# Splitting one 2 MB weight load of a two-layer encoder block into twelve transfers of few rows

## The reference, cut to what matters

```python
def clamped_swiglu(h):
    glu, lin = jnp.split(h, 2, axis=-1)
    ...
    return glu * jax.nn.sigmoid(SWIGLU_ALPHA * glu) * (lin + 1.0)

    def expert_block(args):
        xb, e = args
        return clamped_swiglu(xb @ w1[e] + b1[e]) @ w2[e] + b2[e]
...
h = layer_norm(DEEPNORM_ALPHA * x + mix, ln1_w, ln1_b)
ffn = moe_ffn(h, router_w, router_b, moe_w1, moe_b1, moe_w2, moe_b2)
return layer_norm(DEEPNORM_ALPHA * h + ffn, ln2_w, ln2_b)
```

## Time and profile before

| | |
|---|---|
| median of 3 runs | 1308.47 us (1308.01 to 1309.79) |
| profiled execution, its own time | 1308.29 us |
| its span, first to last instruction | 1306.5 us |
| PE busy | 1251.2 us, 96% of the span |
| read from main memory | 457.54 MB, 351 GB/s over the span |

### The profile page before, as it was taken

The page is one execution under the profiler, slowest core; times in us unless marked ns, Lnnn a source line. Parts: engine busy times, 40 slices in busy tenths (PEclk is TensorE's granted clock), DMA queues, the critical chain, the costliest instruction groups (busy, mean ns, idle before and its releaser), DMA issues.

```text
span 1306.5 us, 15013 instructions
## 1 busy us (share of the span) xinstructions
PE 1251.2 (96%) x6078; PEld 637.7 (49%) x6078; DVE 453.9 (35%) x911; ACT 218.9 (17%) x427; POOL 3.5 (0%) x17
## 2 busy tenths in 40 slices
PE   9999999999999999999998999999999899999995
PEld 8888888998753333433333333333333333333331
DVE  4999915456357132121221212122121212122123
ACT  1622124131041101101011010101101010111101
POOL 0000000000000000000000000000000000000000
PEclk9999999999999999999999999999999999999999
DMA  9443334326779899999999999999999999999995
GB/s 369 176 158 129 128 131 164 125 98 237 288 306 420 358 433 432 432 431 430 428 430 430 431 431 431 430 431 432 431 432 432 431 429 430 429 432 428 428 424 222
DMA packets 29277, 459.53 MB, mean 352 GB/s; under 512 B 4480, under 2 KB 4864, under 8 KB 9248
## 3 DMA queue, kind: packets, MB, share of 16 engines
q1 hardware_dynamic: 25936, 454.04, 83.1%
q10 hardware_dynamic: 3280, 4.56, 1.1%
HBM read 457.54 MB, written 1.05 MB: 351 GB/s over the span
## 4 chain that ended last, share of the span: by engine, by line
PE 67%; DMA 21%; DVE 9%; ACT 1%; issue 1%; SPq 0%; DVEq 0%
DMA store<-in_moe_w 21%; PE banks L1189 16%; PE banks L796 15%; PE banks L1219 12%; PE banks L810 4%; PE banks L1195 3%; DVE store L1854 2%; PE banks L1071 2%; PE banks L1276 2%; PE banks L1121 2%; DVE store L1851 1%; DVE store L1848 1%; DVE store L1853 1%; ACT store L693 1%; PE banks L1205 1%; PE banks L939 1%
## 5 line engine op out<-in xcount | busy, mean ns | idle before, releaser
L1189 PE MATMUL banks<-store 128*64 128x512 f32 x1536 | 346.6, 600 | 23.5 <-DMA store<-in_moe_w 20.0
L1189 PEld LDWEIGHTS banks<-store 128*64 128x64 f32 x1536 | 111.4, 138 | 241.6 <-issue 213.0
L1219 PE MATMUL banks<-store 128*64 128x512 f32 x960 | 212.6, 595 | 0.0
L796 PE MATMUL banks<-store 128*128 128x256 f32 x896 | 196.7, 380 | 0.0
L796 PEld LDWEIGHTS banks<-store 128*128 128x128 f32 x896 | 169.6, 190 | 25.9 <-issue 3.4
L1848 DVE TENSOR_SCALAR store<-banks 128x512 f32<-128x512 f32 x32 | 22.1, 692 | 441.8 <-PE banks L1195 441.8
L1219 PEld LDWEIGHTS banks<-store 128*64 128x64 f32 x960 | 66.3, 137 | 144.2 <-issue 119.9
L1195 PE MATMUL banks<-store 128*64 128x512 f32 x512 | 116.9, 599 | 0.3 <-DMA store<-in_moe_w 0.3
L693 ACT ACTIVATE store<-store 128x512 f32<-128x512 f32 x30 | 18.9, 630 | 457.6 <-DVE store L1848 457.6
L1862 DVE COPY store<-banks 64x512 f32<-64x512 f32 x30 | 20.8, 694 | 206.8 <-PE banks L1219 206.8
L1121 PEld LDWEIGHTS banks<-store 128*128 128x128 f32 x480 | 57.0, 191 | 26.7 <-issue 23.5
(11 more groups left out here) (368 smaller groups left out, 833.5 us busy)
## 6 DMA issues: line engine op xcount, KB each, us to landing
store<-in_moe_w SPq DMA_DIRECT2D x78, 4096.0 KB, 34.7
store<-in_moe_w SPq DMA_DIRECT2D x32, 2048.0 KB, 16.3
store<-in_w_in SPq DMA_DIRECT2D x30, 1024.0 KB, 5.0
store<-in_w_branch SPq DMA_DIRECT2D x8, 1024.0 KB, 4.8
store<-in_moe_w SPq DMA_DIRECT2D x8, 1024.0 KB, 37.9
store<-in_w_out SPq DMA_DIRECT2D x4, 1024.0 KB, 6.1
store<-in_xT SPq DMA_DIRECT2D x2, 512.0 KB, 5.6
store<-in_w_in SPq DMA_DIRECT2D x2, 512.0 KB, 7.0
```

The lines of the kernel that those rows point to most:

```text
L796: last = mm(b[:, j * SEQ:(j + 1) * SEQ], w[:, k, j * P:j * P + P], xT[:, k, :], start=k == 0, stop=k == KD - 1)
L1189: last = mm(bank[i][64 * ct:64 * ct + 64, :], xg[:, 2 * c + kk, col:col + CAP], w[:, kk, i * FF + ct * 512:i * FF + ct * 512 + 512], start ...
L1219: last = mm(bank[4][64 * dh:64 * dh + 64, :], actT[:, j, 64 * fh:64 * fh + 64], w[:, j, 512 * dh:512 * dh + 512], start=(fh, j) == (0, 0), ...
```

## The change

The load of (31, 0) is issued as twelve transfers in place of one. Ten have six rows each, ten rows apart: rows 0, 10, 20, 30, 40, 50, then rows 1, 11, 21, 31, 41, 51, and so on to rows 9, 19, 29, 39, 49, 59. One has the four rows 60 to 63, one the 64 rows 64 to 127. Together they load the same 2 MB from the same place to the same place. PE's wait for this unit expects twelve times 16 instead of 16. The other loads are as before.

```diff
+        SPREAD = [slice(r, 60, 10) for r in range(10)] + [slice(60, 64), slice(64, P)]
...
             for i, (e, c) in enumerate(TAIL):
                 sp.wait_ge(S["expert_chunk_used"], LAST - NU + i - 2 * NDBL + 1)
-                if c < NW1:
+                if (e, c) == (NE - 1, 0):
+                    for rows in SPREAD:
+                        sp.dma_start(tail_at(e, c)[rows, :], unit_source(e, c)[rows, :]).then_inc(landed[c], 16)
+                elif c < NW1:
                     sp.dma_start(tail_at(e, c), unit_source(e, c)).then_inc(unit_landed[c] if e == NE - 2 else landed[c], 16)
...
             def last_unit(c):
 
-                pe.wait_ge(landed[c], stream_total[c] + 16)
+                pe.wait_ge(landed[c], stream_total[c] + 16 * (1 if c else len(SPREAD)))
                 return tail_at(NE - 1, c)
```

## The result

The changed kernel takes 1325.68 us (median of 4 runs, 1325.37 to 1330.28) against 1308.88 us in the comparison's 4 runs of the kernel before. The ratio is 1.0139 (95% interval 1.0127 to 1.0151): slower by 1.4%, some 17 us. The prediction, 1306.0 us, was wrong, and so was its range, which ended at 1313.3. The profiled execution after has a span of 1323.6 us, 17.1 more than before.

What follows compares the result with a forecast made beforehand. The end is set by the latest DMA engine's landing, not by PE. Late engines save four rows, 2.46 us, other costs 0: 1308.29 - 2.46 = 1305.83, with the median 0.18 higher 1306.0 us; range 1305.5 to 1313.3.

Steps and rivals of the forecast that it cites:

- the issues: On SP, twelve issues of 0.34 us, 4.1 us in all, would delay (31, 1) by 0.7 us, hidden: cost 0.
- What is late next: At the DMA-bound start 1286.19, moved to 1283.73, the landing still decides by 0.04 us; last half has 0.7 to spare.
- The source of the lag: Instruction fetches on the DMA engines: 34 packets, 1.2 us each, 5.1 us per engine if eight alone carry them.
- The row's price: A 16 KB row of the split unit costs one engine 0.616 us; upper bound 1.23; wrong above 0.795.
- The upper bound of +6.5 us: At 1.23 us a row, the busiest engines' 15 rows end 6.5 us past the late engines' old place.
- slack: The busiest engines' seven extra rows, 4.31 us, are paid from their 7.0 us lead over the latest.
- theory A: From the experiments, not the prediction: engines writing the same group of on-chip partitions take turns, about 1.2 us a row.
- Which six engines: The ten six-row transfers always take the same six engines, all early; then the gain stands at 2.46 us.
- second sign of being wrong: The prediction is wrong if one of the four busiest engines, those with 15 rows, is late.
- wrong engines: Rival: one of the four 15-row engines is late, so every later landing is 4.31 us later: 1312.8; chance 0.11.
- contention: Rival: dearer rows, up to 1.23 us, put the busiest engines' landings later: +4.3 us, 1312.8; chance 0.22.
- It cancels: Rival: late engines lose in waiting at the same on-chip places what they save in rows: 1308.5 (1307.3 to 1311.0); chance 0.20.

Runs made afterwards that it cites:

- e8: Changed kernel with (31, 0) as sixteen transfers instead (32 rows four apart, each in four 4 KB pieces): 1308.73 us against 1307.87 for the kernel before, ratio 1.0007.
- e9: Loads only, computation left out: two-row transfers at twelve distances, then split units behind three whole units; with a 6.7 us lag halves took 51.73 us, whole 36.95.
- e1: Loads only, computation left out: groups of 16 KB rows at various places; a unit between whole ones took 25.5 us unsplit, 42.9 with the change.
- e11: Changed kernel with the lower 64 rows as eight transfers of eight rows four apart, upper 64 in one: 1317.52 us against 1308.38 before the change, ratio 1.0075.
- e2: Changed kernel with two transfers of 64 rows in place of the twelve: 1319.19 us against 1307.08 for the kernel before, ratio 1.0090.
- e5: Loads only, computation left out: one split unit between two whole ones each side; without lag whole 25.29 us, halves 30.69, the change 43.59; lag groups set aside.
- e10: Changed kernel leaving out 80 of the unit's 128 rows, the rest as eight transfers of six rows four apart: 1306.77 us in one run against 1308.38.
- e7: Changed kernel leaving out rows 64 to 127, the rest as eight transfers of eight rows four apart: 1306.24 us against 1307.87 before, ratio 0.9995.

## Why the prediction was wrong, point by point

*The frame held.* The end is set by the latest engine's landing; eight engines lead by about 7 us; rows aren't split; the issues are free on SP (e8). *What is late next* was never reached.

*The source of the lag held too.* The prediction called the fetching of instructions a likely source and estimated 1.2 us a packet, 5.1 us an engine. The trace before has the time of each of these packets and each unit's 16 landings. From the unit whose first engine lands at 445.5 us to that at 1253.5, 32 instruction packets pass and the lags of the later eight engines behind the mean of the early eight, summed, grow from 4.3 to 50.1 us: 1.43 us a packet, 5.7 us an engine. The steps are seen one by one: the unit at 1243.7 has a late engine only 5.1 us behind, a packet starts at 1249.5, and at the unit of 1253.5 the least of the late eight is 6.4 behind. The early eight stay within 0.64 us of each other all the while.

*The row's price, the step that failed first.* The prediction took 0.616 us, "because ten rows apart the six rows go to different places", with 1.23 as the upper bound, "if two engines always take turns". That the usual price would hold for the split unit rested on no row, and the nearest row, 0.780, was left to the rivals; 0.795 was the price from which the prediction said that it would be wrong. The rows showed 1.17 from 1245 to 1250 us and 1.52 from 1255 to 1260. Two engines do take turns (1.26 to 1.29 in e9), but three and more meet too: sixteen adjacent rows cost 2.13 (e1). And of six rows ten apart, rows 10 and 40 share a way in by the map of e9, and the other engines write at the same ways with their whole units. So the bound of "two take turns" was too low.

*Who pays, the second step that failed.* The upper bound of +6.5 us had only the busiest engines paying, for their 15 rows. All 16 paid: 11.6 us of all engines between 1240 and 1265. The prediction counted the 64-row transfer as four rows for each engine at the usual price; sixteen engines write it into half of the ways, and it costs 9 us by itself (e11). The point is cleanest in e2: no engine carries more rows, and 12 us go.

*The lag is no slack.* The prediction had the lead of the early engines as slack that pays for the change. It paid for nothing, and with halves it is the opposite: with the lag they cost 14.8 us, without it 5.4 (e9, e5). The reason given by theory A, that engines that are ahead write the split unit where others still write whole units, fits this and the wait for (30, 3), but is argued from the map and not seen row by row. But for the change itself, loads only, the lag makes no difference (18.4 us with it, 18.3 without), and no run says why.

*Which six engines.* Called the weakest step, and wrong by one engine: five are early, one late (e10). That one is late was the prediction's second sign of being wrong; whether it is one of the four with 15 rows or of the two with 14, no run shows. The rival "wrong engines" is true beside contention. Against the other late engines, which have 4 rows, it has up to 11 more: 11 x 0.616 = 6.8 us; it comes 7.8 to 7.9 us behind the next.

*The chances.* Contention (0.22) and wrong engines (0.11) were kept as alternatives with 4.3 us each. They add: 9.4 us that all engines share at the deciding landing and 7.8 of the lone engine. Each had a price that was too small, and no case held both; so 17 us lay outside the range.

*It cancels.* The rule of the ways in was weighed as a reason for no gain at all. As a limit e9 bears it out: two engines on one way in get a row through every 0.63 to 0.65 us, no faster than one engine alone. So rows moved to other engines still pass the late engine's way in, and only rows left out (e7, e10) came sooner; no run moved rows without a loss. But "the same bytes left whoever brings them" left out that the ways not in use stand idle meanwhile: with sixteen engines on half of them the rate is 207 GB/s against 431 (e1).

*PE's clock.* The matmuls that follow the two long waits, 6.07 and 6.96 us in which PE stood idle, took 6.08 and 6.28 us in place of 3.65, and the granted clock was 0.56 from 1255 to 1260 and 0.52 from 1270 to 1280, the level of 1.2 GHz for most of it. These 5.1 us cost nothing here: PE waited again later, for a landing, at 1288.63.

*What stays open.* From 1245 us on nearly all rows are dear in the kernel, those of whole units on late engines too, though some of these, by the map, should have their way in to themselves. In e9 rows of engines that met nobody kept 0.611 when only one pair met. How a 64-row transfer is dealt out over the engines, which would decide this, was not found out. Why two of the late engines are among the lower eight isn't shown either.

## What to carry to other kernels

Keep each DMA engine on its own rows: a transfer of 128 rows, or of 32 rows four apart, runs at 0.61 us per 16 KB row, and eight or six rows four apart lost nothing in the kernel (e7, e10). The transfers of 64 adjacent rows, 16 rows 8 apart or adjacent, and 6 rows 10 apart or adjacent made engines share ways into on-chip memory, at 0.90 to 2.13 us a row when alone, and in the kernel the rows around them became dear too. A full queue with engines out of step can make such a meeting dearer (halves: 14.8 us against 5.4), and did not make it cheaper in any run here. And when two rivals rest on independent facts, price their sum too.

## What the runs showed of the hardware that was not expected

A transfer can slow loads issued before it: the unit ahead of the split one was waited for 6.07 us. The engines that lag are not one half: two of the lower eight and six of the upper (e7). Each instruction packet of 16 KB sets one of these eight back by about 1.4 us, and in a stream that keeps all engines full nothing gives it back. Two engines on one way in take 1.26 to 1.29 us a row each (e9), 3 to 6% over twice 0.611. Four on one, by the map of e9, take 2.13 (sixteen adjacent rows, e1), less than four times 0.611.
